# RWKV heads stage of a fused transformer kernel: norms summed per token, the order around the base blocks changed

## The reference

```python
kk = heads(k * k_k)
kk = kk / maximum(sqrt(sum(kk * kk, axis=-1)), 1e-12)       # per head of 64
def direction(dirn):                                        # forward and backward
    y = wkv7_scan(r, decay, kd, v, -kk, kk * a, reverse=(dirn == 1))
    bonus = sum(r * kd * r_k, axis=-1) * v
    return y, bonus
y = y_f + y_b
mean = mean(y, axis=-1); var = mean(square(y - mean), axis=-1)
yn = (y - mean) * rsqrt(var + 64e-5) * lnx_w + lnx_b
out = (yn + bonus_f + bonus_b) * g
```

## Time and profile before

| | us |
|---|---|
| median of 3 runs | 3282.44 |
| lowest and highest | 3268.68, 3282.60 |
| the profiled execution's own time | 3272.29 |
| its span (first to last instruction) | 3270.5 |
| heads stage in it, first to last instruction | 521.1 |

### The profile page before, as it was taken

How to read it: one execution, slowest core, us unless ns; L and a number is a source line. 1 busy time by engine, 2 the same in 40 slices (tenths; PEclk the granted TensorE clock), 3 DMA queues, 4 the chain that set the end, 5 groups by cost and what they waited for, 6 DMA issues and landing times. The chain is left out here.

```text
span 3270.5 us, 55925 instructions
## 1 busy us (share of the span) xinstructions
PE 3020.4 (92%) x23630; PEld 2387.3 (73%) x23630; DVE 1820.7 (56%) x2705; ACT 1351.1 (41%) x2241; POOL 568.7 (17%) x446
## 2 busy tenths in 40 slices
PE   8989999999979999999989999799688888799999
PEld 6757788887746788887668888677476676588887
DVE  6665633445665543445665737564456756457464
ACT  5555322235455322233464424344354544344242
POOL 1000311211000311212001101233233423011010
PEclk9989999999989999999999999999899999899999
DMA  4101333322101323332012323235311111133232
GB/s 148 52 2 67 104 95 97 97 90 84 52 5 64 103 93 96 97 94 70 1 62 94 116 77 103 97 113 191 129 42 38 38 35 41 47 92 107 86 98 83
DMA packets 82330, 261.43 MB, mean 80 GB/s; under 512 B 9633, under 2 KB 13217, under 8 KB 81697
## 3 DMA queue, kind: packets, MB, share of 16 engines
q1 hardware_dynamic: 71424, 236.35, 22.9%
q10 hardware_dynamic: 10656, 21.50, 1.7%
HBM read 236.84 MB, written 20.97 MB: 79 GB/s over the span
## 5 line engine op out<-in xcount | busy, mean ns | idle before, releaser
L1704 DVE TENSOR_TENSOR mlp_w_lo<-mlp_ring,mlp_w_hi 128x1024 fp32r<-128x1024 f32 (+1 forms) x211 | 251.7, 1193 | 574.6 <-ACT mlp_w_hi L1681 574.5
L1681 ACT ACTIVATE mlp_w_hi<-mlp_ring 128x1024 fp32r<-128x1024 f32 (+1 forms) x211 | 213.2, 1011 | 643.9 <-PE ps L1642 639.1
L1704 DVE TENSOR_TENSOR ffn_w_lo<-ffn_ring,ffn_w_hi 128x1024 fp32r<-128x1024 f32 (+3 forms) x172 | 224.2, 1303 | 438.3 <-ACT ffn_w_hi L1681 438.3
L1681 ACT ACTIVATE ffn_w_hi<-ffn_ring 128x1024 fp32r<-128x1024 f32 (+3 forms) x172 | 187.2, 1089 | 480.8 <-PE ps L1642 476.2
L1641 PE MATMUL ps<-mlp_more_parts,mlp_w_hi 128*128 128x512 f32 x952 | 372.8, 392 | 0.0
L1640 PE MATMUL ps<-tiles_parts,mlp_w_hi 128*128 128x512 f32 x832 | 329.7, 396 | 1.1 <-issue 1.1
L1640 PE MATMUL ps<-ffn_x_parts,ffn_w_hi 128*128 128x512 f32 x792 | 312.6, 395 | 18.1 <-DVE ffn_x_parts L2419 14.2
L1642 PE MATMUL ps<-tiles_parts,mlp_w_lo 128*128 128x512 f32 x832 | 327.7, 394 | 0.0
L1640 PE MATMUL ps<-mlp_more_parts,mlp_w_hi 128*128 128x512 f32 x760 | 306.3, 403 | 19.0 <-DVE mlp_w_lo L1704 10.6
L1641 PE MATMUL ps<-ffn_x_parts,ffn_w_hi 128*128 128x512 f32 x792 | 310.4, 392 | 0.0
L1642 PE MATMUL ps<-ffn_x_parts,ffn_w_lo 128*128 128x512 f32 x792 | 310.3, 392 | 0.0
(11 more groups left out here) (510 smaller groups left out, 5925.4 us busy)
## 6 DMA issues: line engine op xcount, KB each, us to landing
ffn_ring<-in_w_ffn_up SPq DMA_DIRECT2D x88, 512.0 KB, 3.6
mlp_ring<-in_w_up SPq DMA_DIRECT2D x64, 512.0 KB, 3.6
mlp_ring<-in_w_down SPq DMA_DIRECT2D x64, 512.0 KB, 3.6
rwkv_keep<-ffn_ring ACTq DMA_DIRECT2D x64, 256.0 KB, 2.5
sq<-rwkv_keep SPq DMA_DIRECT2D x64, 256.0 KB, 2.9
ffn_ring<-in_w_ffn_down SPq DMA_DIRECT2D x16, 768.0 KB, 4.2
in_ring<-in_w_in SPq DMA_DIRECT2D x22, 512.0 KB, 3.6
mlp_ring<-in_w_in SPq DMA_DIRECT2D x22, 512.0 KB, 3.5
```

The source lines that it names most:

```text
L1681: nc.scalar.activation(w.w_hi[:, n % SPLIT, 0:width], w.ring[:, n % RING, 0:width], ACT.Copy).then_inc(s["w_hi_ready"], 1)
L1704: nc.vector.tensor_tensor(w.w_lo[:, n % SPLIT, 0:width], w.ring[:, n % RING, 0:width], w.w_hi[:, n % SPLIT, 0:width].bitcast(F32), ALU.sub ...
```

## The change

- V's transposes (`turn`, KIND_V) become f32 products with a new constant, `centre` (identity less 1/64 within a head), so that v, and with it y, has mean zero per head. The mean's sums and the centring of y fall away. The masks table grows by 128 columns.
- The sums over heads are taken per token: `head_sums` uses each tile of squares as the stationary side and two columns of `head_ones` as the moving side, and gives 128 tokens x 2 heads for each tile, 8 columns in all. VectorE scales (or floors) and inverts these 128 x 8, ScalarE takes the root while it writes it out to 128 x 512 by a broadcast, and `spread_back` transposes the four tiles on TensorE into the bank, from which VectorE multiplies.
- y is squared at k = 4 instead of 20. Both norms' small operations stand at k = 19 on VectorE, the roots at k = 19 and 20 on ScalarE, the products at k = 21 and 22 on VectorE.
- `base_out` stands between turns 6 and 7 instead of behind the first `gram_r`. `var_sums` and `kk_sums` stand directly behind turn 7. `first_terms` and the small operations come before `mr` 0; `mr` 0 and `mr` 1 come before row 1.
- VectorE spreads the first tile's blocks (`x0_first`, behind the last row), GpSimd the other three.
- The decay scans move to k = 30 and 34, GpSimd's subtractions behind them to 32 and 36, the products with K to 37 and 38.

The diff, cut to its core:

```diff
-                        mm = nc.tensor.transpose(m.ps[:, n % 2, kind * P:(kind + 1) * P], src[:, tile_at(t)], m.ident)
+                        if kind == KIND_V:
+                            nc.tensor.matmul(into, src[:, tile_at(t)], centre, start=True, stop=True)
+                        else:
+                            mm = nc.tensor.transpose(into, src[:, tile_at(t)], m.ident)
...
-                def mean_sums(c, main):
-                    nc.tensor.matmul(m.ps[:, 0, :], m.head_ones, y[:], start=True, stop=True).then_inc(s["y_sums"], 1)
+                def head_sums(bank, squares):
+                    for t in range(NT):
+                        mm = nc.tensor.matmul(m.ps[:, bank, 2 * t:2 * t + 2], squares[:, tile_at(t)], m.head_ones[:, ::HD], start=True, stop=True,
+                                              skip_group_check=True)
+                    return mm
+                def spread_back(bank, wide):
+                    for t in range(NT):
+                        mm = nc.tensor.transpose(m.ps[:, bank, tile_at(t)], wide[:, tile_at(t)], m.ident)
+                    return mm
+                def var_sums(c, main):
+                    pe.wait_ge(s["squared"], c + 1)
+                    if main:
+                        pe.wait_ge(s["turned_taken"], 8 * (c + 2) + 8)
+                    head_sums(0, rs).then_inc(s["var_sums"], 1)
...
                                 turn(i, 2 * t + n)
+                            if main and t == NT - 1 and n == 0:
+                                base_out(i)
...
+                    if oldest:
+                        var_sums(i - 2, main)
+                    if new:
+                        kk_sums(i + 1)
                     if old:
                         gram_r(i - 1, 0)
                     if main:
-                        base_out(i)
+                        row_out(i, 1)
                     if old:
                         gram_r(i - 1, 1)
+                    scan_beat(i - 1, MIDDLE)
                     if oldest:
-                        mean_sums(i - 2, main)
-                    scan_beat(i - 1, MIDDLE)
-                    if main:
-                        row_out(i, 1)
+                        var_spread(i - 2)
                     if old:
                         gram_r(i - 1, 2)
-                    if new:
-                        kk_sums(i + 1)
                     scan_beat(i - 1, MIDDLE + 1)
                     if main:
                         row_out(i, 2)
+                    if new:
+                        kk_spread(i + 1)
...
-                    for t in range(NT):
+                    for t in range(1, NT):
                         if main:
                             x0(i, t)
...
-                    if k in (30, 34):
-                        nc.vector.reciprocal(rs[:, part], rs[:, part]).then_inc(s["tail_inverse"], 1)
+                        nc.vector.tensor_scalar(norms[:, OF_Y, :], m.ps[:, 0, 0:2 * NT], 1.0 / HD, GN_EPS, ALU.mult, ALU.add).then_inc(s["var_ready"], 1)
+                        nc.vector.reciprocal(norms[:, OF_Y, :], norms[:, OF_Y, :]).then_inc(s["tail_inverse"], 1)
...
-                    if k in (22, 24):
+                    if k in (30, 34):
                         nc.vector.tensor_tensor_scan(t8[:, GS + d, :], restart[:], turned(L[:, SW + d, :], d), 0.0, ALU.mult, ALU.add).then_inc(s["sums_ready"], 1)
...
+                    if main:
+                        first_terms(i)
+                    beats(MIDDLE)
                     if old:
                         mr(i - 1, 0)
-                    if main:
-                        first_terms(i)
-                    if old:
                         mr(i - 1, 1)
                     if main:
+                        row(i, 1)
                         r_late(i, 0)
-                    beats(MIDDLE)
-                    if main:
-                        row(i, 1)
```

More of the change, by code:

```diff
@@ L33 @@
 RW_CHUNK = 64
+GN_EPS = 64e-5
 RING = 4
@@ L73 @@
 BANDS2_W = 3 * P
-RMASKS, RMASKS_W = columns(("after", HD), ("before", HD), ("upto", HD), ("own", HD), ("eye", RW_BASE), ("merge", RW_LEVELS * HD), ("take", RW_BASE * P), ("row", RW_BASE * P))
+RMASKS, RMASKS_W = columns(("after", HD), ("before", HD), ("upto", HD), ("own", HD), ("eye", RW_BASE), ("merge", RW_LEVELS * HD), ("take", RW_BASE * P), ("row", RW_BASE * P), ("centre", P))
 def constants():
@@ L130, in constants @@
     row, to = np.arange(P)[:, None], np.arange(P)[None, :]
+    r[:, RMASKS["centre"]:RMASKS["centre"] + P] = (row == to) - (row // HD == to // HD) / HD
     for b in range(RW_BASE):
@@ L2636, in base_row, with placed, per_head @@
             return m.ps[:, 5, packed(2, 2)][:, 0:4 * NT * n].rearrange("p (i n) -> p i n", i=4 * NT)
+        def placed(t):
+            blocks = [P, 4, RW_BASE, RW_BASE]
+            into = X[:, t, :, :].rearrange("p i (b n) -> p i b n", b=RW_BASE)
+            solved = X8[:, 4 * t:4 * t + 4, :].unsqueeze(2).broadcast_to(blocks)
+            own = mask("own").rearrange("p (b n) -> p b n", b=RW_BASE).unsqueeze(1).broadcast_to(blocks)
+            return into, solved, own, ALU.mult
+        def per_head(which):
+            return norms[:, which, :].unsqueeze(2).broadcast_to([P, 2 * NT, HD])
         def flat(ap):
@@ L3409, in _ @@
                         row(i, 6)
+                        x0_first(i)
                         bonus(i)
```

113 lines of the change are left out of this document (59 added, 54 removed).

## The result

The changed kernel takes 3330.8 us (median of 4 runs, 3323.0 to 3336.0) against 3280.2 for the kernel before (4 runs on the same chip, 3268.7 to 3282.6). The ratio is 1.0159, with a 95% interval of 1.0126 to 1.0193: 51 us slower, where 3286 was forecast with 3310 as the upper end.

What follows compares the result with a forecast made beforehand. No single engine bounds the heads stage but the order of hand-overs: a steady channel 1.0 + 2.9 - 0.7 - 1.1 = +2.1 us, six +12.6, with edges +9.2; 3281.5 or 3291.6 by base run, middle 3286; range 3256 to 3310.

Steps and rivals of the forecast that it cites:

- half clock spreads: Rival: the granted clock falls in all channels and into the middle, 4 us a channel, about 3310; chance 0.18.
- Turning, +1.0: V's transposes as f32 products cost +0.14 us a turn, unhidden on TensorE: +1.0 us a channel for seven turns.
- Middle, +2.9: End of turn 6 to the last row's addition: fillers leave, narrow sums come in front; +2.9 us, range 1.5 to 3.5.
- T + 16.8: T is the end of turn 6; the last row's addition was forecast 16.8 us after it, T + 13.9 before.
- Seeds, -0.7: First seed starts 2.2 us after the last row instead of 3.0: -0.7 us a channel (-1.1 to -0.1).
- The term for x0_first, 0.8: VectorE's placing of the first seed block, taken as 0.8 us, between 0.42 and 1.4.
- Merges, -1.1: VectorE loses some 6 us of work, ScalarE's list stays; state step comes earlier: -1.1 us a channel (-0.5 to -1.9).
- the reciprocals were the bound: Rival: VectorE bounds the merges, which shrink by up to 5.6 us a channel; about 3255; chance 0.20.
- Edges: Last iteration -4.4 us, the one before -3.0, prologue +1.2, first two channels +2.8 together.
- The last tail: Last iteration, all one chain: mean, centring and reciprocals go, -4.4 us; tail near 6.5 instead of 10.9 us.
- The prologue: Scans start 4 us later behind kk, reciprocals of 3.4 go, GpSimd's chain ends it: +1.2 us (0 to 3).

Runs made afterwards that it cites:

- before_centred: The kernel before with only V's transposes made products with centre, the mean still taken out later; 3279.1 us, 1.0005.
- full_columns: The changed kernel, nothing moved, each product of the norms' sums streaming 128 columns of head_ones instead of 2; 3304.1 us, 1.0094.
- old_order: The changed kernel with base products behind the first gram_r, first base block behind the first mask, narrow sums where the wide sum stood; 3301.6 us, 1.0078.
- before_base_moved: The kernel before with only base products, first row product and first base block placed as in the change, sums still wide; 3282.8 us, 1.0028.
- full_columns_late_spread: old_order with 128-column sums, plus both root spreads moved behind the last row product and VectorE's products with them behind seed blocks; 3300.1 us, 1.0069.
- covered: The changed kernel with two unread 512-column products added per channel, before the narrow sums and behind the first gram_r; 3302.0 us, 1.0076.
- scans_back: The changed kernel with the two scans back at beats 22 and 24 and GpSimd's work at its old beats; 3329.7 us, 1.0158.

## Why the prediction was wrong

**The time.** 3286 was forecast, 3330.8 came, outside the range. The largest part of the miss is a rival that the text had and priced, "half clock spreads", and gave 0.18; its 3310 too is 21 us short, because the merges, which it took over from the forecast, got longer.

**Turning, +1.0: right in its stretch, not in the total.** before_centred shows +0.9 us per steady channel there. Alone it moves the total by only 2 us, which is not told from nothing, so most of it is taken up elsewhere; the sum had counted all of it.

**Middle, +2.9: right at full clock, wrong in taking the full clock for granted.** The hand-made steps came: base products ahead of turn 7, a gap of 0.78 us before the narrow sums (0.8 forecast), 0.22 us a pair, a gap before the second `gram_r`. In full_columns, the same order at a clock of 1.00, turn 6 ends at 2542.7 and the last row at 2559.4: T + 16.7 against T + 16.8. In the changed kernel it was T + 21.2 in the same channel. The step that failed is the clock of this term: the sum adds +2.9 at a clock of 1.00, and the fall got a chance of 0.18 instead of a term. The text knew the condition ("as soon as the clock in the middle, 1.00 now, is under 0.9") and a price of 4 us a channel; all eight middles came under 0.9 (0.64 to 0.89), and the steady ones are 0.9 to 4.5 us longer than in full_columns. Over all eight that is 18 us in the two profiled executions (132.1 against 114.0), and 21 to 27 us in the totals. What misled was the evidence weighed: the 2.29 us gap before the seeds, after which the clock sometimes fell and sometimes didn't, made the waits look like the thing to count. The narrow products were priced for their time alone, 0.22 us a pair whatever the columns, and nothing was asked about the state in which they leave the clock. By old_order, where TensorE does not wait, and full_columns, where it waits as before, it was mostly they; before_base_moved and full_columns_late_spread show that they are not the only way to a fall.

The Trainium skill, "TensorE: Matmul & The Clock Gate", section "HAM oscillation — how this bites in real kernels", puts such falls down to TensorE waiting for data between bursts. covered agrees with it, where added work in and near the gaps kept the clock up. old_order and full_columns speak against it as the whole story: in the first the clock fell with TensorE issuing all the time, in the second it stayed at 1.00 in seven of eight middles with the waits in place.

**Seeds, -0.7: right in size (2.05 us against 2.96), wrong in its credit.** The gain is the scan's leaving; the first seed block on VectorE by itself made the seed 0.24 us later. The term for x0_first, 0.8, was 0.43, at its low bound, although GpSimd was busy for 1.98 us between the last row and the first seed. By the Trainium skill, "SBUF — State Buffer", section "Who interferes with whom", the order of issue decides which of two such operations waits. The trace agrees: x0_first began 0.04 us ahead of GpSimd's first block (2572.12 against 2572.16) and was not slowed, and that block took 0.97 us where the next took 0.72.

**Merges, -1.1: wrong in sign, +1.0 at full clock.** Forecast 20.1 us, measured 22.17 at a clock of 1.00 and up to 25.5 at less. The step that failed is its last sentence, that GpSimd's chain ends 3.5 us later and its consumers "have more than that". They had. But the step did not ask what the chain would then run beside: it lies beside the A products, which take 1.26 and 1.76 us instead of 0.68 each and hold up U. The rest of the step holds: with the scans early and the clock at 1.00 the merges are 20.27, 0.9 under the 21.17 of before, so "the reciprocals were the bound", which had up to 5.6 us for them, is ruled out: VectorE is busy for 11.6 of 20.3 us there instead of 19.6 of 21.2, and the stretch hardly moves. ScalarE's list is the likely limit (15.5 us busy in either case), which no run tested. (The rival's own sum slips: six channels at -2.4 us with the edges as given, -3.4, make -18, not -24, and some 3260, not 3255. Nothing hangs on it.)

**Edges.** The last tail, from y to the gated output, was forecast near 6.5 us instead of 10.9; it is 7.6 (2902.16 to 2909.74). The narrow sums and the spread of that tail run at the lower clock (1.60 and 1.12 us). The prologue, from the stage's start to the first gram, became 3.7 us longer instead of 1.2: there too the A products, with VectorE's BK products behind them, run beside GpSimd (3.04 and 3.41 us for two, where they took 2.36 and 2.34).

**The sum with what was measured.** 9.2 us as forecast, 21 to 27 for the clock, and for the merges +1.0 instead of -1.1, which is 2.1 us in each of six channels, 12.6. Together 43 to 49, where 51 was measured. That it comes so near is in part luck: it still counts the turning in full, and the edges as forecast, though the prologue was 2.5 and the last tail 1.1 us longer than that. By experiments, from the changed kernel down and by the ratios (1.0159, 1.0094, 1.0039, 1.0010): 21 us by the columns, 18 by the order, 9 by the scans' place, and 3 that remain (the interval of the last reaches down to none).

What stays open is why the clock fell in some middles of a kernel and not in others of the same execution, with the same instructions. Nothing here tells where the turning point lies. Nor was it found why late spreads brought it down again, with no narrow product in the kernel.

## What to carry to other kernels

Price a replaced product twice: for its time, and for what it does to TensorE's clock. A product that streams 2 columns took 0.22 us here where one with 128 took 0.24, so the narrow form saved next to nothing, and the wide one with a strided read of its result gave 21 to 27 us back. This is one kernel, and what else lets the clock fall is not known, so look at the clock of each stretch after such a change. When work is moved later on an engine off the path, look not only at who waits for it but at what will run beside it, above all VectorE operations with two SBUF inputs that begin while a GpSimd operation is running: they waited for its end here. And when an undone edit changes nothing, look at the stages before calling it harmless: scans_back hid 18 us of shorter merges behind later seeds and a lower clock.

## What the runs showed of the hardware

- A group of four f32 products (eight instructions) takes 0.88 us to the next start with 2 streamed columns (2554.30 to 2555.18) and 0.97 with 128 (2546.06 to 2547.03), both at full clock.
- In old_order the granted clock fell to the lower level about 3 us after the narrow products began, although TensorE did not wait (in the changed kernel, behind a wait of 0.78 us, 1 to 2 us after): a gram of 32 small products then took 1.13 us instead of 0.69, a zv group 1.97 instead of 1.15, a spread of four transposes 1.09 instead of 0.66.
- With 128 streamed columns instead of 2 in these sums, and nothing else changed, seven of eight middles were at 1.00 instead of none, and in the old order eight instead of four.
- The clock also fell in middles without a narrow product: two of eight in before_base_moved (0.88, 0.78), four of eight in full_columns_late_spread (0.70 to 0.87).
- The same instructions in the same order left middles at 1.00 or at 0.67 within one execution (old_order: 11.5 or 15.5 us).
- Two added 512-column products per channel made a kernel 29 us faster (3302.0 against 3330.8).
- A VectorE product of 128x512 f32 with two SBUF inputs takes 0.68 us where GpSimd is idle. Where a GpSimd operation on SBUF was running when it began, it ended 0.55 us after that operation's end (1.26 and 1.76 us in the channel shown).
- A VectorE product of 128x256 with two SBUF inputs that began 0.04 us before GpSimd's block took 0.43 us; GpSimd's took 0.97 where its next took 0.72.
